# Recurrent heads in another order of work: how the sums are normalized and when each product is issued

## What is computed

```
s = q @ k.T * exp(dmat - m_t)           # per head and direction
num = s @ v (+ what came in before)     # here: one sum over all 768 keys
den = row sums of s (+ the same)
h = num / max(|den|, exp(-m_t))
h_lat = h_forward + h_backward
mix = rmsnorm(h_lat) * g * sigmoid(o)   # mlstm_out
pooled = (mean over a window - u) @ w_pool * scale
x = x + gate * rmsnorm(concat(mix, pooled) @ w_out)
```

## Time and profile before

| | us |
|---|---|
| median of 3 runs | 2998.04 |
| lowest and highest | 2993.45 and 2999.45 |
| the profiled execution, its own time | 2997.43 |
| its span, first to last instruction | 2995.3 |

### The profile page before, as it was taken

How to read it: one execution, slowest core, us unless ns; L and a number is a source line. 1 busy time by engine, 2 the same in 40 slices (tenths; PEclk the granted TensorE clock), 3 DMA queues, 4 the chain that set the end, 5 groups by cost and what they waited for, 6 DMA issues and landing times. The chain is left out here.

```text
span 2995.3 us, 36131 instructions
## 1 busy us (share of the span) xinstructions
PE 2947.4 (98%) x14719; PEld 2485.1 (83%) x14719; DVE 1786.5 (60%) x2589; ACT 1125.8 (38%) x1682; POOL 225.3 (8%) x184
## 2 busy tenths in 40 slices
PE   8999999999999999999999999999999998999999
PEld 6888888888888888888888899888899866788887
DVE  7767566765867767677757655323357756443233
ACT  4433332433424333324424344222235555432222
POOL 0300000000001101100000011000011014100000
PEclk9999999999999999999999999999999999999999
DMA  7454355344433434343443344222235240122221
GB/s 288 154 182 140 128 185 192 127 141 138 143 127 114 162 111 139 99 149 131 148 147 139 122 140 158 97 99 99 97 121 176 87 144 19 57 92 99 99 98 64
DMA packets 108900, 385.78 MB, mean 129 GB/s; under 512 B 12088, under 2 KB 13496, under 8 KB 108736
## 3 DMA queue, kind: packets, MB, share of 16 engines
q1 hardware_dynamic: 83808, 296.36, 29.1%
q10 hardware_dynamic: 24928, 87.12, 8.7%
HBM read 381.32 MB, written 2.11 MB: 128 GB/s over the span
## 5 line engine op out<-in xcount | busy, mean ns | idle before, releaser
L1900 DVE TENSOR_TENSOR WL<-stage,WH 128x1024 fp32r<-128x1024 f32 x508 | 631.8, 1245 | 562.0 <-ACT WH L1252 561.8
L460 PE MATMUL ps<-HH,WH 128*128 128x512 f32 x2184 | 853.5, 391 | 0.9 <-DVE WL L1900 0.9
L461 PE MATMUL ps<-HL,WH 128*128 128x512 f32 x2184 | 850.2, 389 | 0.0
L462 PE MATMUL ps<-HH,WL 128*128 128x512 f32 x2184 | 849.9, 389 | 0.0
L1252 ACT ACTIVATE WH<-stage 128x1024 fp32r<-128x1024 f32 x512 | 537.8, 1053 | 440.0 <-PE ps L462 427.2
L460 PE MATMUL ps<-GH,WH 128*128 128x512 f32 (+2 forms) x1649 | 570.6, 346 | 5.0 <-DVE WL L1890 2.4
L462 PE MATMUL ps<-GH,WL 128*128 128x512 f32 (+2 forms) x1649 | 569.0, 345 | 0.0
L461 PE MATMUL ps<-GL,WH 128*128 128x512 f32 (+2 forms) x1649 | 569.0, 345 | 0.0
L462 PEld LDWEIGHTS ps<-HH,WL 128*128 128x128 f32 x2184 | 410.0, 188 | 85.7
L460 PEld LDWEIGHTS ps<-HH,WH 128*128 128x128 f32 x2184 | 410.2, 188 | 84.4 <-issue 1.9
L461 PEld LDWEIGHTS ps<-HL,WH 128*128 128x128 f32 x2184 | 410.3, 188 | 82.3
(11 more groups left out here) (265 smaller groups left out, 2880.1 us busy)
## 6 DMA issues: line engine op xcount, KB each, us to landing
stage<-ws SPq DMA_DIRECT2D x535, 512.0 KB, 3.3
MST<-wm ACTq DMA_DIRECT2D x154, 512.0 KB, 3.3
Z<-wm SPq DMA_DIRECT2D x10, 512.0 KB, 7.8
TAB<-consts ACTq DMA_DIRECT2D x7, 448.0 KB, 3.6
MST<-wm SPq DMA_DIRECT2D x6, 512.0 KB, 7.1
Z<-max_rows ACTq DMA_DIRECT2D x8, 256.0 KB, 3.4
out<-X SPq DMA_DIRECT2D x8, 256.0 KB, 2.2
X<-xT SPq DMA_DIRECT2D x4, 256.0 KB, 4.9
```

The costliest lines, as they stand in the source:

```text
L460: e.matmul(o, wh, mh, start=start, stop=False, **more)
L461: e.matmul(o, wh, ml, start=False, stop=False, **more)
L462: return e.matmul(o, wl, mh, start=False, stop=stop, **more)
L1900: e.tensor_tensor(wl, src, wh.bitcast(F32), ALU.subtract).then_inc(wlo.sem, wlo.up(("w", i)))
```

## The change

The amount of arithmetic stays the same. The order in the lists of PE, ACT and DVE in this stage is new; POOL's list stays. `sums` takes one or two directions, so that other work can stand between them. `exponents` is split into the columns off the diagonal and `masked_exponents`. Two score products (c of 4 and 5) now stand ahead of `sums(h, 2)`. The normalization no longer goes through `STAT`: ACT copies both accumulators to `SCR` as soon as the head's sums are complete (`sums_out`), PE then spreads the reciprocals into the accumulators' own banks, behind that copy, and DVE multiplies bank and copy. The squares of a head are an ACT step of their own, later in its list (`head_squares`). The weight chunks of the heads are split at one place in each of the first three heads. The third query and key product of head 0 goes to bank 3, and `scores(0, 0)` and `scores(0, 1)` stand between the pooling's products.

```diff
+        def weights_of(h, c, d):
+            return SCR[:, WEIGHED[h, c, d] % 5, :]
+        def weights_free(lane, h, c, d):
+            n = WEIGHED[h, c, d]
+            if n < 5:
+                lane.wait_ge(lo, "u", NH - 1, 1)
+            else:
+                lane.wait_ge(plo, "e", *WEIGHED_OF[n - 5])
+        def sums_of(h, d):
+            return PS[2 * (h % 2) + d]
...
             def scores(h, c):
                 P = score_bank("sc", h, c)
                 if c == 0:
+                    pe.wait_ge(lo, "qk", h, 0)
                     pe.wait_ge(lo, "qk", h, 2)
+                elif c == 2:
+                    pe.wait_ge(lo, "qk", h, 1)
                 done(mm3(P[:, :], *keys(h, c), *slot(12), True, True), ("sc", h, c))
-            def sums(h, c):
-                if c == 0:
+            def sums(h, c, *directions):
+                if c == 0 and 0 in directions:
                     if h == 0:
                         for d in range(2):
                             banks.wait(pe, d)
...
                         pe.wait_ge(lo, "qk", h, 0)
                         sums_bank(h, 1)
                         pe.wait_ge(ev, "den", h - 1)
-                for d in range(2):
+                for d in directions:
...
             def normalize(h, d):
                 pe.wait_ge(dv, "dinv", h)
-                stat_free()
+                pe.wait_ge(ev, "cp", h, d)
                 for t in range(4):
-                    inst = spread(DV[:, 4 * d + t:4 * d + t + 1], t)
+                    inst = e.matmul(sums_of(h, d)[:, t * 128:t * 128 + 128],
+                                    DV[:, 4 * d + t:4 * d + t + 1].to_broadcast([128, 128]), IDN[:, :], start=True, stop=True)
                 done(inst, ("nb", h, d))
-                stat["free"] = (ev, ("nb", h, d))
...
             q_and_k(0, 0, score_bank("qk", 0, 0))
+            q_and_k(0, 1, score_bank("qk", 0, 1))
+            q_and_k(0, 2, PS[banks.put(pe, 3, ("qk", 0, 2), lo, "qk", 0, 2)])
             pool_mean(2)
             pool_out(0)
...
+            scores(0, 0)
             pool_mean(3)
+            scores(0, 1)
             pool_out(1)
             pool_out(2)
...
             def early(*units):
                 for nn, k in units:
...
             beside = [(nn, k) for nn in range(2) for k in (0, 1, 4, 5, 6, 7)]
+            def beside_sums(i):
+                early(*beside[2 * i:2 * i + 2])
             for h in range(NH):
                 more = h + 1 < NH
...
+                if h:
+                    scores(h, 1)
+                    normalize(h - 1, 0)
+                    normalize(h - 1, 1)
+                scores(h, 2)
+                if h == 0:
+                    pool_out(3)
+                sums(h, 0, 0)
+                scores(h, 3)
+                sums(h, 0, 1)
+                sums(h, 1, 0)
+                if h:
+                    head_sums(h - 1)
+                sums(h, 1, 1)
+                if not more:
+                    beside_sums(0)
+                scores(h, 4)
+                scores(h, 5)
+                sums(h, 2, 0, 1)
                 if more:
                     q_and_k(h + 1, 0, sums_bank(h + 1, 0))
                 else:
...
+                    beside_sums(1)
+                sums(h, 3, 0)
+                if h:
+                    rms_last(("hn", h - 1), S, dv, "hn1", h - 1)
+                sums(h, 3, 1)
                 if more:
                     q_and_k(h + 1, 1, score_bank("qk", h + 1, 1))
+                else:
+                    beside_sums(2)
+                    beside_sums(3)
+                sums(h, 4, 0)
+                if more:
                     q_and_k(h + 1, 2, score_bank("qk", h + 1, 2))
                 else:
...
+                    beside_sums(4)
+                sums(h, 4, 1)
+                if not more:
+                    beside_sums(5)
+                sums(h, 5, 0, 1)
                 if more:
                     scores(h + 1, 0)
...
                 denominators(h)
             early((0, 2), (1, 2))
...
+            def exponents(h, c, d):
+                a, b = spans(c, d)
+                _, rest = diagonal(c, d, b - a)
+                if rest.stop > rest.start:
+                    weights_free(act, h, c, d)
                     act.wait_ge(*max_landed(h, d))
...
+                    act.wait_ge(dv, "gct")
+                    e.activation(weights_of(h, c, d)[:, rest], maximum(h, d)[:, a:b][:, rest], ACT.Exp, scale=-1.0,
+                                 bias=GC[:, c, 32 * d + h:32 * d + h + 1]).then_inc(ev.sem, ev.up(("e", h, c, d)))
+            def masked_exponents(h, c, d):
+                a, b = spans(c, d)
+                dd, _ = diagonal(c, d, b - a)
+                T = weights_of(h, c, d)
+                act.wait_ge(dv, "g1", h, c, d)
+                e.activation(T[:, dd], T[:, dd], ACT.Exp, scale=-1.0).then_inc(ev.sem, ev.up(("e", h, c, d)))
+            def weigh(h, c, d):
+                a, b = spans(c, d)
+                n = WEIGHED[h, c, d]
+                act.wait_ge(dv, "sc", h, c, d)
+                if n >= 4:
+                    act.wait_ge(mm, "sum", *WEIGHED_OF[n - 4])
+                else:
+                    act.wait_ge(mm, "pm", 3)
+                high(GH[:, 14 + n % 4, 0:b - a], weights_of(h, c, d)[:, 0:b - a], "e", h, c, d)
...
+            def sums_out(h, d):
+                act.wait_ge(mm, "sum", h, 5, 1)
                 T = SCR[:, 5 + sn.take(act, ("dn", h, d), *((lo, "mix", h) if d == 0 else (dv, "hh", h))), :]
-                e.activation(T, STAT[:, :], ACT.Copy).then_inc(ev.sem, ev.up(("nb", h, d)))
-                if d:
-                    act.wait_ge(dv, "hh", h)
-                    act.wait_ge(mm, "ss", ("hn", h - 1) if h else ("an", 1, 1))
-                    e.activation(SSQ[:, :], SN("dn", h, 0), ACT.Square).then_inc(sq.sem, sq.up(("hn", h)))
+                e.activation(T, sums_of(h, d)[:, :], ACT.Copy).then_inc(ev.sem, ev.up(("cp", h, d)))
+            def head_squares(h):
+                act.wait_ge(dv, "hh", h)
+                act.wait_ge(mm, "ss", ("hn", h - 1) if h else ("an", 1, 1))
+                e.activation(SSQ[:, :], SN("dn", h, 0), ACT.Square).then_inc(sq.sem, sq.up(("hn", h)))
...
             q_and_k(0, 0, score_bank("qk", 0, 0))
+            q_and_k(0, 2, PS[3])
+            q_and_k(0, 1, score_bank("qk", 0, 1))
             weights(("pm", 3), ahead=-1)
             pool_mean(2)
             pool_out(0)
...
+            exponents(0, 1, 0)
+            exponents(0, 1, 1)
+            weigh(0, 0, 0)
             pool_mean(3)
+            weigh(0, 0, 1)
+            pool_out(1)
             for h in range(NH):
                 more = h + 1 < NH
...
+                if h:
+                    exponents(h, 1, 0)
+                    weigh(h, 0, 0)
+                    exponents(h, 1, 1)
+                    weigh(h, 0, 1)
+                exponents(h, 2, 0)
+                weigh(h, 1, 0)
+                exponents(h, 2, 1)
+                masked_exponents(h, 2, 0)
+                masked_exponents(h, 2, 1)
+                weigh(h, 1, 1)
+                if h == 0:
+                    pool_out(2)
+                exponents(h, 3, 0)
+                if h:
+                    head_squares(h - 1)
+                exponents(h, 3, 1)
+                if h == 0:
+                    pool_out(3)
+                weigh(h, 2, 0)
+                masked_exponents(h, 3, 0)
+                masked_exponents(h, 3, 1)
+                weigh(h, 2, 1)
                 if more:
...
+                    weights(("po", 3), ahead=h + 1)
+                weigh(h, 3, 0)
+                exponents(h, 4, 0)
+                weigh(h, 3, 1)
+                exponents(h, 4, 1)
+                masked_exponents(h, 4, 0)
+                masked_exponents(h, 4, 1)
+                masked_exponents(h, 5, 0)
+                exponents(h, 5, 1)
+                weigh(h, 4, 0)
+                masked_exponents(h, 5, 1)
+                weigh(h, 4, 1)
+                if 0 < h < NH - 1:
+                    for d in range(2):
+                        running_max(h + 1, d)
+                if more:
+                    q_and_k(h + 1, 0, sums_of(h + 1, 0))
+                weigh(h, 5, 0)
+                weigh(h, 5, 1)
+                if more:
                     q_and_k(h + 1, 1, score_bank("qk", h + 1, 1))
                     q_and_k(h + 1, 2, score_bank("qk", h + 1, 2))
...
+                    exponents(h + 1, 0, 0)
+                if h:
+                    head_norm(h - 1)
+                if more:
+                    exponents(h + 1, 0, 1)
                 denominators(h)
+                sums_out(h, 0)
+                sums_out(h, 1)
             weights(("early", 1, 7), ahead=2)
...
             weights(("early", 2, 7))
+            head_squares(NH - 1)
...
                 T = SN("dn", h, d)
-                dve.wait_ge(ev, "nb", h, d)
-                dve.wait_ge(mm, "sum", h, 5, 1)
```

(65 more changed lines are left out.)

165 lines of the change are left out of this document (30 added, 135 removed).

## The result

The changed kernel takes 2979.36 us (median of 6 runs, 2978.02 to 2979.67) where the kernel before takes 2997.18 beside it (6 runs, 2993.35 to 3001.69): a ratio of 0.9938, interval 0.9928 to 0.9948. Forecast were 2979.0. The profiled execution took 2978.02 us, its span is 2976.1 against 2995.3. Beside the last experiments the kernel was run again: 2979.63, ratio 0.9939 (0.9926 to 0.9951). The kernels of the experiments ran on three chips, each group beside the kernel before, so a ratio can be compared between groups; a time in us only within one.

A forecast was written before the change was run, and what follows sets the result against it. PE was taken as bound by latency of lists blocking each other, not by a rate. Head gains 3.5 + 6.2 + 7.9 + 0.8 = 18.4 us off 2997.43 gave 2979.0; range (8 in 10) 2972 to 2992.

The forecast's parts named there:

- A steady head: Heads 1 and 2: 21.4 us of PE products plus 1.0 wait before `scores(h, 5)`, 22.4; gains 6.2 and 7.9.
- The mechanism: Four-head stage: strictly ordered lists block each other, no engine's rate binds; 15.5 us PE idle, 6.6 at lower clock.
- Normalization: Accumulator copies and reciprocal spreads: early copy removes PE's 0.6 us and DVE's 7.1 of waits, already in the heads' sums.
- Head 0: First head: idle 2.4 before `pool_out(3)`, 0.6 before `scores(0, 2)`, 1.1 before `scores(0, 5)`, clock 0.7; total gain 3.5 us.
- The 0.5 in front: Before the first head: three query and key products cover a weight part PE reached too early; gain 0.5 us.
- Head 3: Last head: 1.3 us idle and 0.3 restarts now; transposes then wait 0.6 for ACT's |den|; gain 0.8.
- The running maximum: Its two loads, moved behind tile 4's high parts, land in 3.0 to 3.4 us: zero cost, 0.6 us cover.
- Rival A: DVE becomes the bound through SBUF collisions with POOL: DVE 22.6 us, heads 25, gain 11, 2986.5; chance 0.20.
- A reading of the earlier trace: Head 1 restart cost: a sum begun at 2481.73 ends in a stall, restarting at 2485.23 with a 0.51 matmul, usually 0.40.
- B: ACT and DVE lists block each other at new places; only 0.6 and 1 to 2 us won, 2995.5; chance 0.08.
- C: `scores(h, 5)` ahead of ready `sums(h, 2)` waits for late weighings; 8 us late in heads 0-2 gives 3003; chance 0.06.

The follow-up runs named there:

- the kernel with the gap removed: The changed kernel with `pool_out(3)` of head 0 behind the first sum and fourth score product on PE: 2980.98 us, ratio 0.995.
- the last version: The changed kernel with DVE's weight part, head 0's pooled outputs and a high part, maximum loads and one next-product block moved: 2975.30 us, ratio 0.9924.
- the route alone: The kernel before with only the normalization changed (early accumulator copies, reciprocals spread into the accumulators' banks), lists otherwise old: 2991.44 us, ratio 0.9983.

## Why the prediction was right, and where it was not

- *A steady head: right.* The sum said 22.4 us, 21.4 of products and a wait of 1.0 before `scores(h, 5)`. The profile shows 22.26 and 22.33 with waits of 1.08 and 1.07, and two kernels, one with DVE's part later and one with more in front, move this wait down to nothing and up by what was added. In total the forecast was nearer than its parts: the stage gave 19.5 us and not 18.4, while the medians differ by 17.8, less than the profiles.
- *The mechanism: right.* The loss was in lists that block each other. With ACT's and DVE's lists (and PE's) in the new order and the old route the stage gains 16.9 of 19.5 us; with PE's list alone, 0.8. What ACT's list and DVE's list give one by one is open.
- *Normalization: mis-sized.* The step that said that it takes PE's 0.6 us and DVE's 7.1 of waits, "both already in the heads' sums", was right for the sum, but I took the route for a small part by itself. Alone it gives 6.5 us of the stage and 5 of the time. It keeps DVE from standing in front of weighings, and the low clock of heads 1 and 2 goes with PE's stalls. That the clock follows from the stalls is read from the profiles and not shown by a run of its own. The other lists' order takes most of the same waits away, so it adds only 2.6.
- *Head 0: right by luck, by errors that cancel.* The gap was 2.17 (2.4 forecast), the wait before `scores(0, 2)` 0.17 and not 0.6, the one before `scores(0, 5)` 0.43 and not 1.1, while the slow matmuls took 1.6 and not 0.7. So PE's idle time in the head fell by 2.5 us and not by 1.3, and at the lower clock next to nothing. The 0.5 in front didn't come as it was meant: PE stood nowhere in that stretch, and the wait of 0.41 for DVE's weight part just before the stage's first product is there before and after. The errors behind the gap are one thing: a wait that ends when DVE is done shrinks by what was lost ahead of it. My sum added gap, clock and wait as if each cost by itself; the kernel with the gap removed shows that the first two cost nothing.
- *Head 3: mis-sized.* 1.7 and not 0.8. The last gap of 1.05 before a sum is gone and a wait of 0.68 for |den| has come, as forecast (0.6). But the restarts were more than the one that I counted: the timeline of before has six matmuls of 0.50 us and three of 0.48 in this head, where 0.40 is usual, that of after one of 0.50 and five of 0.45 to 0.48. PE's busy time fell by 1.1 as well (27.88 to 26.74); these matmuls are less than half of that, the rest is open.
- *The running maximum: mis-sized, without effect.* Forecast were 3.0 to 3.4 us to landing and 0.6 of cover. The profile of after has, for the four loads from 2440 us on, `DMA to landing us min/median/max: 3.7/4.0/4.4`: the weight chunks of a head now load in the same time (DMA share 0.18 where the earlier trace rows have 0.07), which is the likely reason; no run tests it. The cover is gone and ACT stood 0.31 twice, in front of exponents that nobody needed yet.
- *Rival A: its mechanism is there, its count is not.* The masks take 0.547 us in the mean instead of 0.474, the sum of the directions 0.90 in the mean, where the pair of the earlier trace rows has 1.32 and 0.69:

```profile
L2621 DVE SCALAR_TENSOR_TENSOR SCR<-Z,GC,TAB 128x128 f32<-128x128 f32 x24 | 12.4, 547 | 0.0
L2651 DVE TENSOR_TENSOR SCR<-SCR 128x512 f32<-128x512 f32 x3 | 2.7, 901 | 0.7 <-DVE SCR L2645 0.5
```

DVE works 19.24 us in head 1, 1.2 more than before and not 4.5. The eight masks of the head take 4.27 instead of 3.82. The weight part is 1.25 more: before, it stood in the stretch of head 0, so the 18.07 from which rival A was added up held none. It took 1.25 and not 2.07 because POOL had all but stopped. Rival A charged every operation with two SBUF inputs for a meeting; in these lists 13 of 24 masks and all weight parts (1.22 to 1.27) were not held up. DVE is 90% busy in heads 1 and 2 of the last version (19.48 of 21.57 us), and they are 21.6 long and not 25.
- *A reading of the earlier trace rows: wrong, without effect.* The restart at 2485.23 doesn't follow the sum that began before 2481.73. Between them stands a score product that began at 2482.82, behind a wait and with a restart of its own. Six stalls of head 1 were counted all the same, and there are six.

- *Rivals B and C: didn't come.* No wait of B's kind stayed. C's mechanism costs some 0.5 us in all.

What stays open: why the slow matmuls come at a place in one kernel and not in another. In head 0 they stood behind a gap of 2.17 in after, behind a wait of 2.04 in the kernel with late work on DVE, but neither behind the same gap of 2.2 with the weight part later nor behind the wait of 2.79 with the pooled output moved.

## What to carry to other kernels

Where no engine but PE is near full and yet PE waits, look for an instruction that stands at the head of its list waiting for what isn't urgent, with ready and urgent work behind it, and write the lists out in time from the durations of the trace: by hand this gave heads 1 and 2 within 0.2 us. Ask for each wait what would end it; if that is another engine's list, the idle time and the slow matmuls ahead of it are free, and removing them wins nothing until that list is shortened ahead of the point. Then move work behind the point and leave the waiting engine's order as it is: DVE's one weight part moved by two places won 0.8 us in each steady head and 3.0 of the profiled stage, PE's product moved won 0.5. And before you charge an operation for an engine that it may collide with, look in time whether the two meet.

## What the runs showed of the hardware

- A DVE product with both inputs in SBUF that began beside one of POOL's back-to-back low parts took 1.19 us, 0.69 alone, and 0.68 beside POOL with one input in a bank. It ended 0.56 after the low part that ran when it began, and the low part behind it took 1.75 instead of 1.29. A mask, a form with two SBUF operands and a scalar, took 0.34 alone and up to 1.11 when a low part ran as it began (heads 1 to 3).
- The granted clock of the stage's heads 1 and 2 was 0.94 and 0.89 of full before and 1.00 with PE's waits at 1.1 us, but also with 3.5 us of short waits in a head (the route alone). Where it fell to the lower of its two levels, 1.2 of 2.4 GHz, matmuls of 512 columns started 0.43 instead of 0.23 us apart; in head 0 there were six to fourteen of them in one spell, and none in three of the kernels.
- A load of the running maximum landed in 3.7 to 4.4 us in after (3.6 to 4.8 in its second profile), with weight chunks loading in the same stretch, and in 3.0 to 3.4 before.
